# A two-layer decoder trunk on one core: four of every sixteen gathered expert rows are added by VectorE, twelve are summed by TensorE

## The reference, cut to what matters

```python
def peer_ffn(x, w_query, sub_keys, expert_u, expert_v):
    ...                                    # 8 heads; 16 experts of 16384 chosen per token and head
    idx = jnp.take_along_axis(cidx, sel, axis=-1)
    gate = jax.nn.softmax(top_s, axis=-1)
    def block(args):
        xb, ib, gb = args
        pre = jnp.einsum('td,thkd->thk', xb, expert_u[ib])
        act = jax.nn.gelu(pre.astype(jnp.float32), approximate=False) * gb
        return jnp.einsum('thk,thkd->td', act.astype(xb.dtype), expert_v[ib])
```

## Time and profile before

| | us |
|---|---|
| median of 3 runs | 3619.2 |
| lowest, highest | 3610.1, 3627.41 |
| the profiled execution's own time | 3624.84 |
| its span, first to last instruction | 3622.6 |
| busy: PE / DVE / POOL / ACT | 2871.8 / 2196.6 / 1392.2 / 760.8 |
| mean granted TensorE clock | 0.958 of full speed |

### The profile page before, as it was taken

One profiled execution on the slowest core, in us unless ns is written; L12 is line 12 of the kernel. 1 busy time (PEld: TensorE's weight loads), 2 busy tenths in 40 slices (PEclk: granted clock), 3 DMA queues, 4 the chain that ended last, 5 costly groups with the idle time before them and its releaser, 6 DMA issues.

```text
span 3622.6 us, 31542 instructions
## 1 busy us (share of the span) xinstructions
PE 2871.8 (79%) x10443; PEld 1662.0 (46%) x10443; DVE 2196.6 (61%) x3080; ACT 760.8 (21%) x1189; POOL 1392.2 (38%) x1028
## 2 busy tenths in 40 slices
PE   7999938878787788777789999388777877787776
PEld 7887824433342343232388778234333423332322
DVE  6765576665656566655566655765656655665655
ACT  4344411111111111111143444011111111111111
POOL 0000046545545555544400000555545555555443
PEclk9999969999999999999999999699999999999999
DMA  5434579999999999999944344899999999999998
GB/s 190 142 127 150 197 284 408 414 418 413 416 419 414 404 419 419 415 416 415 420 145 141 127 165 161 338 411 417 414 412 411 419 421 408 415 416 418 413 419 362
DMA packets 239655, 1243.78 MB, mean 343 GB/s; under 512 B 24680, under 2 KB 33072, under 8 KB 107440
## 3 DMA queue, kind: packets, MB, share of 16 engines
q0 software_dynamic: 147456, 1073.81, 72.1%
q1 hardware_dynamic: 92080, 168.51, 13.6%
HBM read 1240.14 MB, written 2.10 MB: 343 GB/s over the span
## 4 chain that ended last, share of the span: by engine, by line
DMA 36%; PE 32%; DVE 17%; issue 8%; DVEq 3%; ACT 2%; POOL 2%; POOLq 0%; SPq 0%; ACTq 0%
DMA work<-in_peer_v_dram,idx_v 21%; PE PS L502 16%; DMA work<-in_peer_u_dram,idx_u 14%; PE PS L801 13%; DVE work L1702 6%; POOL work L1140 2%; DVE xs L1715 2%; DVE lo L1268 2%; DVEq L1379 1%; ACT hi L860 1%; DVE gain L1646 1%; DVE gain L1647 1%; ACT work L934 1%; DVE gain L1680 0%; DVE gain L1649 0%
## 5 line engine op out<-in xcount | busy, mean ns | idle before, releaser
L801 PE MATMUL PS<-work,diag 128*128 128x512 f32 x3968 | 1855.5, 615 | 640.0 <-DMA work<-in_peer_v_dram,idx_v 455.9
L1702 DVE CUSTOM_DVE_ANT_0 work<-work,hn 128x2048 f32<-128x2048 f32 x512 | 1164.3, 2291 | 851.2 <-DMA work<-in_peer_u_dram,idx_u 820.7
L801 PEld LDWEIGHTS PS<-work,diag 128*128 128x128 f32 x3968 | 739.6, 195 | 1726.0 <-issue 1302.8
L1140 POOL DMA_INDIRECT work<-in_peer_u_dram,idx_u x512 | 775.4, 1514 | 1501.2 <-DVEq L1686 941.6
L1140 POOL DMA_INDIRECT work<-in_peer_v_dram,idx_v x512 | 616.6, 1204 | 700.0 <-PE PS L801 565.4
L1069 ACT ACTIVATE diag<-cst,act_k 128x128 f32<-128x128 f32 x496 | 190.1, 398 | 1383.9 <-PE PS L801 1374.0
L502 PE MATMUL PS<-hT_hi,hi 128*128 128x256 f32 x1024 | 306.6, 299 | 43.8 <-DVE lo L1602 16.2
L502 PE MATMUL PS<-hT_lo,hi 128*128 128x256 f32 x1024 | 295.8, 289 | 0.0
L502 PE MATMUL PS<-hT_hi,lo 128*128 128x256 f32 x1024 | 295.7, 289 | 0.0
L502 PE MATMUL PS<-hi,hT_hi 128*128 128x512 f32 (+1 forms) x704 | 278.5, 396 | 9.9 <-ACT work L904 4.1
L502 PE MATMUL PS<-hi,hT_lo 128*128 128x512 f32 (+1 forms) x704 | 272.1, 386 | 0.0
(11 more groups left out here) (251 smaller groups left out, 1615.1 us busy)
## 6 DMA issues: line engine op xcount, KB each, us to landing
raw<-in_w_in_dram SPq DMA_DIRECT2D x40, 1024.0 KB, 5.0
gain<-in_w_in_dram SPq DMA_DIRECT2D x38, 1024.0 KB, 5.0
raw<-in_peer_query_dram SPq DMA_DIRECT2D x24, 1024.0 KB, 16.1
raw<-in_w_out_dram SPq DMA_DIRECT2D x16, 1024.0 KB, 5.1
gain<-in_w_out_dram SPq DMA_DIRECT2D x16, 1024.0 KB, 5.1
work<-in_peer_query_dram SPq DMA_DIRECT2D x8, 1024.0 KB, 7.4
work<-in_peer_u_dram,idx_u POOLq DMA_INDIRECT x512, 14.3
work<-in_peer_v_dram,idx_v POOLq DMA_INDIRECT x512, 14.0
```

What stands on the lines that cost most here:

```text
L801: mm = pe.matmul(PS[:, j, :], diag[:, n % RING, :], vrow[n % RING][:, j * 512:(j + 1) * 512], start=(k == 0), stop=(k == (TOPK - 2 if last ...
L1140: pool.indirect_dma_start(out=dst, out_offset=None, in_=tables[table], in_offset=bass.IndirectOffsetOnAxis(ap=idx, axis=0)).then_inc(loade ...
L1702: dve.tensor_tensor_reduce(r, r, hn[:, b, :], 1.0, 0.0, ALU.mult, ALU.add, pre[:, b, k:k + 1]).then_inc(u_free.sem, 1)
```

## The change

In groups of 16 rows the rows k = 3, 7, 11 and 15, which are those that land in the last buffer of the v ring, are no longer multiplied by a diagonal on TensorE. VectorE multiplies them by their weight and adds them to x itself (`add_v`, one `scalar_tensor_tensor` over 2048 columns). TensorE sums the other twelve; ScalarE writes no diagonal for the four. A new semaphore `v_added` frees the last buffer. The `add_v` calls stand at fixed places among the dots; the last group of each layer keeps its own scheme.

```diff
+ADDED_SLOT = RING - 1
+ADDED = [k for k in range(TOPK) if k % RING == ADDED_SLOT]
+SUMMED = [k for k in range(TOPK) if k % RING != ADDED_SLOT]
...
-                        for k in range(TOPK):
+                        for k in SUMMED:
                             sum_rows(h, 0, k)
...
-                    row("v", idx_v[b][:, k:k + 1], vrow[k % RING], v_free, g * TOPK + k - RING + 1, v_loaded[k % RING])
+                    if k in ADDED:
+                        row("v", idx_v[b][:, k:k + 1], vrow[k % RING], v_added, g * NADD + ADDED.index(k), v_loaded[k % RING])
+                    else:
+                        row("v", idx_v[b][:, k:k + 1], vrow[k % RING], v_free, g * NSUM + SUMMED.index(k) - RING + 2, v_loaded[k % RING])
...
+                def add_v(h, b, k):
+                    g = h * NB + b
+                    dve.wait_ge(v_loaded[k % RING].sem, (l * V_TURNS + g * (TOPK // RING) + k // RING) * 16 + 16)
+                    r = xs[:, b, :]
+                    dve.scalar_tensor_tensor(out=r, in0=vrow[k % RING], scalar=act_k[:, b, k:k + 1], in1=r, op0=ALU.mult, op1=ALU.add)
+                    dve.drain().then_inc(v_added.sem, 1)
...
                 def dve_head(h, r, i=None):
                     dots(h, 1, range(0, 2))
                     ...
-                    dots(h, 1, range(2, 8))
+                    dots(h, 1, range(2, 5))
+                    add_v(h, 0, 3)
+                    dots(h, 1, range(5, 8))
                     choose(h + 1, 0)
                     v_indices(h, 1)
-                    dots(h, 1, range(8, TOPK))
+                    dots(h, 1, range(8, 9))
+                    add_v(h, 0, 7)
+                    dots(h, 1, range(9, 13))
+                    add_v(h, 0, 11)
+                    dots(h, 1, range(13, TOPK))
+                    add_v(h, 0, 15)
                     activate(h, 1)
                     take_sum(h, 0)
                     dots(h + 1, 0, range(0, 2))
                     ...
-                    dots(h + 1, 0, range(2, 6))
+                    dots(h + 1, 0, range(2, 5))
+                    add_v(h, 1, 3)
+                    dots(h + 1, 0, range(5, 6))
                     choose(h + 1, 1)
                     v_indices(h + 1, 0)
-                    dots(h + 1, 0, range(6, 13))
+                    dots(h + 1, 0, range(6, 9))
+                    add_v(h, 1, 7)
+                    dots(h + 1, 0, range(9, 13))
+                    add_v(h, 1, 11)
                     ...
                     dots(h + 1, 0, range(13, TOPK))
+                    add_v(h, 1, 15)
                     activate(h + 1, 0)
                     take_sum(h, 1)
```

More of the change, by code:

```diff
@@ L75 @@
 U_TURNS, V_TURNS = U_ROWS // RING, V_ROWS // RING
-LAST_V = (GROUPS - 1) * TOPK
+ADDED_SLOT = RING - 1
+ADDED = [k for k in range(TOPK) if k % RING == ADDED_SLOT]
+SUMMED = [k for k in range(TOPK) if k % RING != ADDED_SLOT]
+NSUM, NADD = len(SUMMED), len(ADDED)
+LAST_V = (GROUPS - 1) * NSUM
+V_SUMS, V_ADDS = LAST_V + TOPK // 2, (GROUPS - 1) * NADD
 CONST = {}
@@ L359, in trunk @@
         u_free = signal("u_free", U_ROWS, start=RING)
-        v_free = signal("v_free", V_ROWS, start=RING)
+        v_free = signal("v_free", V_SUMS, start=RING - 1)
+        v_added = signal("v_added", V_ADDS, start=1)
         dotted = signal("dotted", GROUPS)
@@ L363, in trunk @@
         act_ready = signal("act_ready", GROUPS)
-        diag_ready = signal("diag_ready", V_ROWS)
+        diag_ready = signal("diag_ready", V_SUMS)
         sum_taken = signal("sum_taken", GROUPS, start=1)
@@ L793, in sum_rows @@
                     g = h * NB + b
-                    n = k // 2 if last else k
+                    n, i = (k // 2, k // 2) if last else (k, SUMMED.index(k))
                     if k == 0:
                         pe.wait_ge(sum_taken.sem, sum_taken.upto(l, g))
-                    pe.wait_ge(diag_ready.sem, diag_ready.upto(l, g * TOPK + n + 1))
+                    pe.wait_ge(diag_ready.sem, diag_ready.upto(l, g * NSUM + i + 1))
                     pe.wait_ge(v_loaded[n % RING].sem, (l * V_TURNS + g * (TOPK // RING) + n // RING) * 16 + 16)
                     for j in range(4):
-                        mm = pe.matmul(PS[:, j, :], diag[:, n % RING, :], vrow[n % RING][:, j * 512:(j + 1) * 512],
-                                       start=(k == 0), stop=(k == (TOPK - 2 if last else TOPK - 1)))
+                        mm = pe.matmul(PS[:, j, :], diag[:, i % RING, :], vrow[n % RING][:, j * 512:(j + 1) * 512],
+                                       start=(k == 0), stop=(k == (TOPK - 2 if last else SUMMED[-1])))
                     mm.then_inc(v_free.sem, 1)
@@ L1065, in diagonals @@
                     for k in ks:
-                        n = k // 2 if last else k
-                        act.wait_ge(v_free.sem, v_free.upto(l, g * TOPK + n - RING + 1))
+                        if not last and k not in SUMMED:
+                            continue
+                        n = k // 2 if last else SUMMED.index(k)
+                        act.wait_ge(v_free.sem, v_free.upto(l, g * NSUM + n - RING + 1))
                         act.activation(diag[:, n % RING, :], ident, ACT.Copy, scale=act_k[:, b, k:k + 1]).then_inc(diag_ready.sem, 1)
@@ L1162, in fetch_last @@
                     if k % 2 == 0:
-                        row("v", idx_v[NB - 1][:, k:k + 1], vrow[i], v_free, LAST_V + n - RING + 1, v_loaded[i])
+                        if n == ADDED_SLOT:
+                            row("v", idx_v[NB - 1][:, k:k + 1], vrow[i], v_added, V_ADDS, v_loaded[i])
+                        else:
+                            row("v", idx_v[NB - 1][:, k:k + 1], vrow[i], v_free, LAST_V + (n - RING + 2 if n < RING else n - RING + 1), v_loaded[i])
                     else:
@@ L1192, in bc @@
                 return ap.to_broadcast(shape)
-            for s in (u_free, v_free, gain_used, wq_lo_ready, small_used, top_taken, vidx_ready, sum_taken):
+            for s in (u_free, v_free, v_added, gain_used, wq_lo_ready, small_used, top_taken, vidx_ready, sum_taken):
                 dve.sem_inc(s.sem, s.start)
@@ L1711, in take_sum @@
                 def take_sum(h, b):
-                    dve.wait_ge(v_free.sem, v_free.upto(l, (h * NB + b + 1) * TOPK))
+                    dve.wait_ge(v_free.sem, v_free.upto(l, (h * NB + b + 1) * NSUM))
                     dve.tensor_tensor(xs[:, b, :], xs[:, b, :], bank(0, 4), ALU.add)
@@ L1718, in take_last_sum @@
                 def take_last_sum():
-                    dve.wait_ge(v_free.sem, v_free.upto(l, V_ROWS))
+                    dve.wait_ge(v_free.sem, v_free.upto(l, V_SUMS))
                     for o in range(NO):
@@ L1769, in _ @@
                 v_indices(HEADS - 1, 1)
-                dots(HEADS - 1, 1, range(8))
+                dots(HEADS - 1, 1, range(0, 5))
+                add_v(HEADS - 1, 0, 3)
+                dots(HEADS - 1, 1, range(5, 8))
                 if l + 1 < DEPTH:
                     split_piece(l + 1, 0)
-                dots(HEADS - 1, 1, range(8, TOPK))
+                dots(HEADS - 1, 1, range(8, 9))
+                add_v(HEADS - 1, 0, 7)
+                dots(HEADS - 1, 1, range(9, 13))
+                add_v(HEADS - 1, 0, 11)
+                dots(HEADS - 1, 1, range(13, TOPK))
+                add_v(HEADS - 1, 0, 15)
                 activate(HEADS - 1, 1)
```

## The result

The changed kernel takes 3674.8 us (median; 3670.6 to 3678.3) against 3621.1 for the kernel before: the ratio is 1.0152, with a 95% interval of 1.0131 to 1.0172. It is slower by 1.5%, some 54 us. The forecast was 3684, or 65 us more.

A forecast was written before the change was run, and what follows sets the result against it. Transfers were taken to set the pace, with no slack around `choose` in half A. The profiled execution's 3624.8 + 69 - 4 = 3690 us, or 3684 in terms of the median; range 3632 to 3722.

The forecast's parts named there:

- The turn of the loop: Four groups, from one `take_sum` to the same one a turn later: 334.4 us would become 343 us.
- Add 7 in half A: Behind `choose` and dot 8, it delays v11 by about 4.9 us at 14 places: 69 us (49 to 94).
- The missing gather: During `choose` in half A, v11 cannot go out, so the queue holds one gather less: 2.49 us.
- Half B: `choose` after dot 5: u10 blocks there and v11 does not wait for add 7; cost 0, at most 2.35 us.
- Group end: At `take_sum`, the wait for v15 replaces the wait for TensorE: 0.5 us earlier, 2 us gained over 4 places.
- The relief: 2 us at group ends plus 2 us from TensorE working off its lag behind query pieces sooner: -4 us.
- TensorE's clock: Pauses from omitted rows slow four rows a group by 1.7 us each, at no cost; granted clock somewhat below 0.97.
- Rival 3: TensorE's clock stays low, rows take up to 7.3 us: +540 us, 4160 us; chance 0.03.
- rival 2: No change: gathers still in flight cover the gap at v11, relief pays the rest: 3619 us, within 18; chance 0.13.
- rival 4: Each half B loses an add as well, POOL being held up behind `choose`: 33 us more, 3717 us; chance 0.12.

The follow-up runs named there:

- relief alone: Kernel before, with TensorE summing only the first 512 of 2048 columns of rows 3, 7, 11 and 15 and no adds on VectorE: 3617.1 us, ratio 0.9990.
- row 3 twice: Changed kernel with the add of row 3 in half A made twice, so that row counts double in x: 3675.5 us, ratio 1.0153.
- rows 2, 6, 10, 14: Changed kernel adding the third buffer's rows instead, each right after its dot, with key scores one row earlier on TensorE: 3622.1 us, ratio 1.0008.
- row 7 small, in place: Changed kernel with row 7's add in half A cut to 16 of 2048 columns, still behind `choose` and dot 8: 3647.4 us, ratio 1.0073.
- small, ahead: Changed kernel with row 7's add in half A cut to 16 columns and placed ahead of `choose`, after dot 7: 3623.9 us, ratio 1.0008.
- whole, ahead: Changed kernel with the full add of row 7 in half A placed ahead of `choose`, right after dot 7: 3655.2 us, ratio 1.0096.
- `choose` cut in two: Kernel before, with `choose` split and dot 8 (half A) or dot 6 (half B) between its parts: 3613.5 us, ratio 0.9986.

## Why the prediction was right

**What sets the pace.** The transfers do. Three quarters of every fourth row sum taken off TensorE change the time by 4.6 us in all (relief alone), adds on VectorE in the pause for the next landing by nothing that can be told (row 3 twice; rows 2, 6, 10, 14). What counts is when the gathers around `choose` go out. The turn of the loop was put at 343 us and measured 341.2.

**Add 7 in half A.** This was the term that I said would decide, and it did. Placed before `choose` as a small add, the version is at 1.0008; left where it is, at 1.0152. That difference is 51 us, where the prediction had 69. Made small in its place, the add gave back 2.0 us a place; made twice, it cost 2.25 more, against the 2.35 of its length. The missing gather is the 23 us between the two small adds, 1.7 us a place against 2.49. The timelines of the profiled executions show it at the place itself. Below is how long after dot 7 the later dots start, in us, as a mean of the 14 halves A with a `choose`; at the pace of 4.98 it would be 24.9 and 39.8.

| | before | changed | row 7 small, in place | small, ahead | whole, ahead | k = 2, 6, 10, 14 |
|---|---|---|---|---|---|---|
| dot 12 | 25.56 | 29.74 | 27.58 | 25.24 | 26.58 | 25.05 |
| dot 15 | 40.77 | 44.97 | 43.00 | 40.74 | 43.39 | 40.08 |

**The mis-sized term.** It is the loss at each half A, for which I took 4.9 us. It measured 4.2 (44.97 - 40.77), 59 us in 14 places against 69. What was off is not where the changed kernel ends up: by my numbers dot 12 would start 762.8 + 2.5 - 735.5 = 29.8 us after dot 7, and it starts at 29.74. It is where the kernel before stood. I read one half A, that of the earlier trace rows, in which dot 12 came 25.0 us after dot 7, and concluded that nothing was lost; over all 14 it comes at 25.56 (24.83 to 26.38), so 0.7 us were lost already. Why is not shown: with `choose` cut in two it is still 25.46.

That the 29.8 was met is in part luck, since two of its terms were off and cancelled. I took 8.1 to 8.2 us from issue to landing with an empty queue, and v11 took 7.0 on average (6.8 to 7.4). I let u12 land 2.5 us behind it, and it landed 3.3 behind it, 7.6 us after its own issue. For the v11 of the half A shown above the trace gives:

```profile
DMA to landing us min/median/max: 6.9/6.9/6.9
```

**Half B** moved neither way, as said: its v11 did not wait for the add. **Group end**: the wait for v15 took the place of the wait for TensorE, 0.85 us shorter where I had said 0.5. But nothing was gained by that: from dot 15 of a half B to dot 7 of the next half A it takes 42.7 us on average, where it took 42.3 before.

**The relief** of 4 us in the sum does not show in the trace of the changed kernel. The relief alone measured 4.6, but that is TensorE's part without adds, and not the same thing. In the two profiled executions, 53.5 us apart, the 69 became 59, and the -4 became about +1 for all other stretches from dot 0 of a layer's second group to dot 0 of its last. Some 6 us the other way lie in the first group of each layer: it takes 47.5 and 46.4 us in the changed kernel, 50.1 and 49.6 in the kernel before. The change does nothing there, and in the profiled executions of seven of the other versions this group takes 45.3 to 52.6 us. That looks like scatter between executions, which is not shown further, and it was luck that it made up for the relief. Differences of a few us, such as the 2 us by which k = 2, 6, 10, 14 lies above the kernel before, are not explained here.

**TensorE's clock** fell by more than "somewhat": 0.97 to 0.83 in the PEER windows. The slow rows show it, here three rows in 13.72 us where they took 11.0, after a pause of 10.95 us; the windows behind the timeline's line are of its beginning, at a granted clock of 0.50, the lower of the two levels, and of its end, at 1.00:

```profile
774.48 13.72 PE L807 MATMUL PS<-work,diag 128*128 128x512 f32 x24 [10.95 <-DMA work<-in_peer_v_dram,idx_v]
...
776.00:778.00 2.00, 2.00 (x3) 0.67 (x2) 1.05 (x1) 0.00 (x0) 1.58 (x2) 0.50 0.99 418
782.00:784.00 2.00, 2.00 (x6) 0.85 (x5) 2.00 (x1) 0.00 (x0) 0.00 (x0) 1.00 1.04 438
```

It is the first half of the rule that the prediction cited ("TensorE: Matmul & The Clock Gate", the section on the HAM clock gate, in the Trainium skill: idleness puts the array back to half rate), and the trace agrees by these 13.72 us and the 0.50. One forecast failed here: TensorE's busy time was to fall by over 400 us and fell by 239 (2871.8 to 2633.2). The page of the kernel before has 3968 matmuls of row sums in 1855.5 us, that of the changed kernel 3008 in 1613.5: the 960 that went were worth 449 us, but those that stayed took 207 us longer. My own four slow rows of 1.7 us in each of 30 groups make 204, and I had left them out of that figure. The cost in time was nothing that can be told, as forecast: the versions at 1.0008 run at granted clocks of 0.84 and 0.85 in that stretch. Rival 3 did not come about: the clock came back within a group. Neither did rival 2, since the queue ran dry, nor rival 4, since half B did not pay.

## What to carry to other kernels

Where transfers set the pace, as here, ask of each buffer in a ring who releases it and what stands ahead of that release on its engine: a release moved behind a long block of other work shortens the queue by one transfer for the whole block, and an in-order issuer holds up everything behind it. Work moved to an engine that waits for data is free in the pause for the next landing and paid in full next to the block that already uses up the slack: the same 2.35 us cost 0 in one place and 2.2 in the other. To find such a place, compare the last issue before the block and the first behind it with the pace of the landings, and do so at all its occurrences: one of them had nothing lost where the mean of 14 had lost 0.7 us. The busy shares do not show it.

## What the runs showed of the hardware that was not expected

The granted TensorE clock reacted strongly to the loss of every fourth row, 0.97 to 0.83 in the PEER windows, and filling three of the pauses in a group with equal work brought the span's mean back only from 0.856 to 0.887; neither moved the time the way that a bound by TensorE would have. When v11 was issued into the empty queue, data moved again 3.0 us after the start of the issuing instruction on POOL (761.40 to about 764.4), and the gather had landed after 6.9 us; over the 14 places it was 6.8 to 7.4. That instruction took 2.43 us beside the dots of VectorE; the v11 that went out during `choose` in the kernel before took 0.94.
